# Stick-breaking attention: the sums over later key blocks formed on VectorE, and one product with the matrix of ones per block

## The reference, cut to what matters

```python
z = einsum('bhtd,bhsd->bhts', q, k) * scale          # t: query, s: key
mask = (s_idx < t_idx) & (s_idx >= pad)
log_beta = log_sigmoid(z)
log_rest = where(mask, log_sigmoid(-z), 0.0)
later = cumsum(log_rest, axis=keys, reverse=True) - log_rest   # sum over the keys after s
att = where(mask, exp(log_beta + later), 0.0)
out = einsum('bhts,bhsd->bhtd', att, v)
```

## Time and profile before

| | |
|---|---|
| median of 3 runs | 1735.72 us (1735.57 to 1742.43) |
| profiled execution | 1740.51 us, span 1738.4 us from first to last instruction |
| TensorE products (PE) | busy 1616.3 us, 93% of the span, 16180 instructions |
| DVE, ACT, POOL | 810.9 us (47%), 610.9 us (35%), 162.9 us (9%) |
| attention's pairs | 34 us each while there is fill, seven of them; the eighth has none |

### The profile page before, as it was taken

One profiled execution on the slowest core, in us unless ns is written; L12 is line 12 of the kernel. 1 busy time (PEld: TensorE's weight loads), 2 busy tenths in 40 slices (PEclk: granted clock), 3 DMA queues, 4 the chain that ended last, 5 costly groups with the idle time before them and its releaser, 6 DMA issues. The chain is left out here.

```text
span 1738.4 us, 35740 instructions
## 1 busy us (share of the span) xinstructions
PE 1616.3 (93%) x16180; PEld 1459.7 (84%) x16180; DVE 810.9 (47%) x1098; ACT 610.9 (35%) x827; POOL 162.9 (9%) x186
## 2 busy tenths in 40 slices
PE   4999998899999999979999979888669999999997
PEld 3999987899999999979998968887438888888885
DVE  3455445154442344456766535445485444334432
ACT  2445435242221222236567332233243333122321
POOL 2001001001100011300000321101030010001100
PEclk9999999799999999998999979999889999999998
DMA  3221120122332233332222110000103333323331
GB/s 100 68 62 44 56 64 30 49 86 87 97 105 78 86 89 103 97 116 79 81 70 60 45 52 4 5 4 4 49 22 87 95 90 112 91 86 97 96 99 49
DMA packets 214167, 121.35 MB, mean 70 GB/s; under 512 B 8744, under 2 KB 209600, under 8 KB 213760
## 3 DMA queue, kind: packets, MB, share of 16 engines
q1 hardware_dynamic: 213712, 118.98, 23.3%
q10 hardware_dynamic: 304, 0.08, 0.0%
HBM read 112.29 MB, written 6.76 MB: 68 GB/s over the span
## 5 line engine op out<-in xcount | busy, mean ns | idle before, releaser
L125 ACT ACTIVATE w_hi<-w_raw 128x1024 fp32r<-128x1024 f32 (+1 forms) x194 | 215.9, 1114 | 600.0 <-PE psg L732 481.0
L732 PE MATMUL psg<-x_hi,w_hi 128*128 128x264 f32 (+1 forms) x1096 | 357.2, 326 | 9.3 <-PEq L2469 9.3
L732 PE MATMUL psg<-x_lo,w_hi 128*128 128x264 f32 (+1 forms) x1096 | 357.2, 326 | 0.0
L732 PE MATMUL psg<-x_hi,w_lo 128*128 128x264 f32 (+1 forms) x1096 | 356.4, 325 | 0.0
L129 DVE TENSOR_TENSOR w_lo<-w_raw,w_hi 128x1024 fp32r<-128x1024 f32 (+1 forms) x194 | 250.4, 1291 | 145.5 <-ACT w_hi L125 145.5
L732 PEld LDWEIGHTS psg<-x_hi,w_hi 128*128 128x128 f32 x1096 | 206.2, 188 | 28.8 <-issue 10.3
L732 PEld LDWEIGHTS psg<-x_lo,w_hi 128*128 128x128 f32 x1096 | 206.2, 188 | 18.1 <-issue 0.2
L732 PEld LDWEIGHTS psg<-x_hi,w_lo 128*128 128x128 f32 x1096 | 206.6, 189 | 17.5
L732 PE MATMUL psg<-mid_hi,w_hi 128*128 128x264 f32 (+1 forms) x451 | 146.5, 325 | 0.0
L732 PE MATMUL psg<-mid_lo,w_hi 128*128 128x264 f32 (+1 forms) x451 | 146.3, 324 | 0.0
L732 PE MATMUL psg<-mid_hi,w_lo 128*128 128x264 f32 (+1 forms) x451 | 145.9, 323 | 0.0
(11 more groups left out here) (367 smaller groups left out, 3370.6 us busy)
## 6 DMA issues: line engine op xcount, KB each, us to landing
w_raw<-in_w_ffn_in_dram SPq DMA_DIRECT2D x88, 512.0 KB, 3.8
w_raw<-in_w_ffn_out_dram SPq DMA_DIRECT2D x32, 704.0 KB, 4.6
w_raw<-in_w_qkv_dram SPq DMA_DIRECT2D x24, 512.0 KB, 3.7
w_raw<-in_w_rkv_dram SPq DMA_DIRECT2D x24, 512.0 KB, 3.8
w_raw<-in_w_o_attn_dram SPq DMA_DIRECT2D x8, 512.0 KB, 4.1
w_raw<-in_w_o_rwkv_dram SPq DMA_DIRECT2D x8, 512.0 KB, 3.8
v_first<-v_pair SPq DMA_DIRECT2D x8, 264.0 KB, 2.1
res_kept<-res SPq DMA_DIRECT2D x1, 2112.0 KB, 7.8
```

Source lines behind the costliest of these rows:

```text
L125: k.nc.scalar.activation(k.w_hi[j][:, 0:kt, :], k.raw[j][:, 0:kt, :], ACT.Copy).then_inc(k.hi_ready[j].h, 1)
L732: done = k.nc.tensor.matmul(k.psg[:, 2 * j + c, 0:size], w[:, t, :], x, start=t == first and n == 0, stop=t == last and n == 2)
```

## The change

The far columns of rest are used once more. After rest_low(p, hp) has taken its parts, DVE adds block 4's 16 columns onto the last 16 of block 3, then block 3's 144 onto the last of block 2, then block 2's 272 onto the last of block 1, in place (`later_keys`). Each far block of rest then holds, key by key, the sum over itself and all later blocks. ACT rounds these 864 columns into sum_hi (`sums_high`), DVE makes sum_lo (`sums_low`). TensorE's `later` is cut in two: `own_block` has the products with tri as before, `later_blocks` has for each of four blocks one product with minus on the summed block that follows it, hi and lo, 8 products in place of 20. It waits for sum_lo. Both heads' `own_block` come first, then both heads' `later_blocks`. The diff, with the declarations of semaphores and tiles left out:

```diff
+        def sums_high(p, hp):
+            act.wait_ge(self.add_r.h, 3 * (2 * p + hp + 1))
+            if p:
+                act.wait_ge(self.later_d.h, 2 * (p - 1) + hp + 1)
+            nc.scalar.activation(b.sum_hi[hp][:], b.rest[hp][:, 512:SCORES], ACT.Copy).then_inc(self.shi_r.h, 1)
...
             rest_high(p, 1, 0)
             rest_high(p, 1, 1)
+            sums_high(p, 0)
+            sums_high(p, 1)
...
+        def later_keys(p, hp):
+            n = 2 * p + hp
+            at = [piece_cols(a).start for a in (1, 3, 4, 5)]
+            dve.wait_ge(self.rlo_far.h, n + 1)
+            for step, (to, width, skip) in enumerate(((2, 16, 128), (1, 144, 128), (0, 272, 128))):
+                if step:
+                    dve.wait_ge(self.add_r.h, 3 * n + step)
+                own = b.rest[hp][:, at[to] + skip:at[to] + skip + width]
+                nc.vector.tensor_tensor(own, own, b.rest[hp][:, at[to + 1]:at[to + 1] + width], ALU.add)\
+                    .then_inc(self.add_r.h, 1)
+
+        def sums_low(p, hp):
+            dve.wait_ge(self.shi_r.h, 2 * p + hp + 1)
+            nc.vector.tensor_tensor(b.sum_lo[hp][:], b.rest[hp][:, 512:SCORES], b.sum_hi[hp][:].bitcast(F32),
+                                    ALU.subtract).then_inc(self.slo_r.h, 1)
...
             rest_low(p, 0)
+            later_keys(p, 0)
             softplus(p, 1, 1)
             rest_low(p, 1)
+            later_keys(p, 1)
+            sums_low(p, 0)
+            sums_low(p, 1)
...
-        def later(p, hp):
+        def own_block(p, hp):
...
-            for a, (bank, col, width, key, t0) in enumerate(PIECES):
-                for c, (_, _, width2, key2, t2) in enumerate(PIECES):
-                    if key2 > key and a != 2:
-                        at = col + t2 - t0
-                        for r in (b.rest_hi[hp], b.rest_lo[hp]):
-                            done = mm(ps[:, bank, at:at + width2], b.minus[:], r[:, piece_cols(c)], start=False, stop=True,
-                                      skip_group_check=True)
+        def later_blocks(p, hp):
+            ps = (k.psg, k.psx)[hp]
+            pe.wait_ge(self.slo_r.h, 2 * p + hp + 1)
+            for a, c in ((0, 1), (1, 3), (3, 4), (4, 5)):
+                bank, col, width, key, t0 = PIECES[a]
+                _, _, width2, _, t2 = PIECES[c]
+                at, cols = col + t2 - t0, piece_cols(c)
+                for r in (b.sum_hi[hp], b.sum_lo[hp]):
+                    done = mm(ps[:, bank, at:at + width2], b.minus[:], r[:, cols.start - 512:cols.stop - 512], start=False,
+                              stop=True, skip_group_check=True)
             done.then_inc(self.later_d.h, 1)
...
-            later(p, 0)
-            later(p, 1)
+            own_block(p, 0)
+            own_block(p, 1)
+            later_blocks(p, 0)
+            later_blocks(p, 1)
```

More of the change, by code:

```diff
@@ L200, in __init__ @@
          self.xl_r, self.sq_r, self.acc_r, self.sum_d, self.rs_r, self.half_d, self.half_r, self.z_d, self.clip_r,
-         self.exp_r, self.ln_r, self.rest_r, self.rhi_r, self.rlo_near, self.rlo_far, self.later_d, self.att_r, self.vt_d,
+         self.exp_r, self.ln_r, self.rest_r, self.rhi_r, self.rlo_near, self.rlo_far, self.later_d, self.whole_r, self.add_r, self.shi_r, self.slo_r, self.att_r, self.vt_d,
          self.vt_r, self.out_d, self.ohi_r, self.olo_r, self.v_saved) = (
@@ L205, in __init__ @@
                 "sum", "rstd", "half", "half_read", "z", "clipped", "exp", "ln", "rest", "rest_hi", "lo_near", "lo_far",
-                "later", "att", "v_turned", "v_tok", "out", "o_hi", "o_lo", "v_saved"))
+                "later", "read", "summed", "sums_hi", "sums_lo", "att", "v_turned", "v_tok", "out", "o_hi", "o_lo", "v_saved"))
     def memory(self):
@@ L223, in memory @@
         b.rest_hi, b.rest_lo = ([area.tile(f"rest_{x}{n}", [P, SCORES], F32R) for n in range(2)] for x in ("hi", "lo"))
+        b.sum_hi, b.sum_lo = ([area.tile(f"sum_{x}{n}", [P, SCORES - 512], F32R) for n in range(2)] for x in ("hi", "lo"))
         b.att = b.rest
```

## The result

| | before | changed |
|---|---|---|
| median of 6 runs, us | 1739.86 (1735.57 to 1746.88) | 1768.76 (1760.19 to 1772.22) |
| ratio, 95% interval | | 1.0145 (1.0112 to 1.0177): slower |
| span of the profiled execution | 1738.4 | 1768.7 |
| seven pairs with fill / last pair / all behind attention | 234.6 / 38.7 / 1409.5 | 262.3 / 35.5 / 1414.4 |

The last row is read from the timelines of the one profiled execution of each kernel: a pair reaches from its first product of z to that of the next. The prediction was 1742 us, in a range of 1725 to 1752; the measured 1768.76 lies outside. By the ratio the change costs 25 us (under 2%, but clear of the noise) where 6 were forecast.

The account below looks back on a forecast made before the run. TensorE was taken to bound attention, busy 34.00 of 34 us at full clock. Gains of 8.8 us against 15 us lost to clock falls gave +6 us on 1735.7, so 1742 us, range 1725 to 1752.

Parts of the forecast that it names:

- Part 1: TensorE in attention: 8 minus products a head for 20 remove 2.76 us a middle pair, 5.18 in the last, without waits.
- Part 2: VectorE in attention: three adds a head of 0.17, 0.31 and 0.45 us start the pair's last softplus 1.02 us later.
- Part 3: Middle pairs: TensorE waits 1.82 us for the second head's rest_lo, leaving 0.63 us gain a pair, 4.4 over seven.
- Part 4: Last pair, without fill and at half clock: a gain of 4.4 us, 5.18 less a wait of 0.78.
- Part 5: TensorE's clock in the seven pairs: the wait makes it fall in five, 3.0 us each, 15 us lost.
- rival (b): Seven attention pairs: the clock falls in all at 4.8 us each, +25 us net, 1761 us; chance 0.12.

Follow-up runs that it names:

- e3: The changed kernel with 24 more, useless projection products between the two own blocks in each of seven pairs; 1736.16 us, ratio 0.9984 to the kernel before.
- e2: The changed kernel with POOL's rest_lo of the second head waiting for the first head's three adds; 1757.58 us, ratio 1.0102 to the kernel before.
- e4: The kernel before with only the product order changed: both own blocks first, then all twenty minus products of each head, no adds; 1746.43 us, ratio 1.0036.
- e1: The changed kernel with the first head's adds moved behind the second head's rest_lo on VectorE; 1739.97 us, ratio 1.0003 to the kernel before.
- e6: The changed kernel with the whole half of 24 projection products between the two own blocks, adds left early; 1740.39 us, ratio 1.0000 to the kernel before.
- e8: The changed kernel with adds and sums computed but unused, TensorE running the twenty old products a head in old order; 1741.18 us, ratio 0.9996 to the kernel before.
- e5: e1 with 15 of the 24 projection products that followed the minus products moved between the two own blocks; 1721.80 us, ratio 0.9866 to the kernel before.
- e10: e5 with the first head's adds put back early, beside POOL's rest_lo; 1737.12 us, ratio 0.9968 to the kernel before.
- e7: e6 with the first head's adds behind the second head's rest_lo; 1741.95 us, ratio 0.9995 to the kernel before.

## Why the prediction was wrong

**Part 1 (what TensorE loses) held.** In e3, at full clock, the eight products of a head take 1.08 and 1.09 us (109.22 to 110.30, to 111.39), where the twenty took 2.42 and 2.44: 2.69 us less; 2.76 was forecast.

**Part 2 (the shift by the adds) failed.** Each add alone was priced right (0.17, 0.31, 0.45 against 174, 307, 441 ns) and so was the shift of 1.02 us: it is 1.02 in e2 (from 0.97 to 1.99 us between rest_lo and the softplus, 103.92 to 105.91). In the changed kernel it is 2.01 (105.47 to 108.45). The step that failed is the price of the first head's adds: the prediction asked what they wait for and not what runs beside them. POOL's rest_lo was in the trace of before, then beside a softplus with one operand in PSUM. The rows from which the adds were priced (434 ns for 256 columns) show nothing of this, but the same trace has it in the RWKV stage:

```profile
1028.67 0.68 DVE L2090 TENSOR_TENSOR ar<-xn,w_ext 128x512 f32<-128x512 f32 x1
1028.69 1.78 POOL L2070 TENSOR_TENSOR bk<-kk_in,w_inv 128x512 f32<-128x512 f32 x1
1029.27 1.77 DVE L2091 TENSOR_TENSOR ar<-rr,w_ext 128x512 f32<-128x512 f32 x1
```

L2091 takes 0.68 us where POOL is idle. Of the two operations with both inputs in SBUF here the one that started before POOL's took its usual time and POOL's 0.5 us longer (1.78; it is 1.28 elsewhere); the one that started in the midst of it took 1.77 us and ended 0.57 us after it.

**Part 3 (the wait) had the right place and mechanism**: the second own block waits for rest_lo, 0.80 us by the order (e4: 0.76). Its size was forecast as 1.82 us from the end of the first own block; on the same measure it was 2.81 (111.69 less 107.23, less the 1.65 that the block takes), 0.99 more, which is what Part 2 missed (2.01 less 1.02). (The sum is off by a trifle: 108.65 and the 1.05 us of the second head's products make 109.70 and not 109.75, so 0.68 us a pair and not 0.63.) So what was to be a gain of 0.63 us a pair is a loss of 0.26 (e3) even at full clock.

**Part 4 (the last pair)**: 4.4 us of gain forecast, 3.2 found, 4.7 in e2 and 5.7 in e1: the same term.

**Part 5 (the clock) was mis-sized in both factors.** Five falls at 3.0 us were forecast, 15 us; in the profiled execution it was seven at 3.7, 26 us. The price of 4.8 for the full case was near what e2 shows for its long kind, 4.5. Together: at full clock the stage should have won 8.8 us and wins 1.4 (3.2 less 7 x 0.26), 7.4 us of the miss; the falls are 11 us of it. That makes the 18.5 us between +6 and the +24.5 measured on the eight pairs. Of the other 8 us between the forecast of 1742 and 1768.8, 4 are the base, whose median was 1735.7 us in three runs and is 1739.9 in six; the rest is near the 4.9 us that what lies behind attention took longer in the profiled execution, for a reason that stays open. The forecast's own range was too narrow by the prediction's own terms: it names 3 to 7 falls of 2 to 4.8 us and ends at 1750, but seven at 4.8 make 1761, the time of rival (b), which the outer range of 1725 to 1752 leaves out too.

The rival (b), +25 us, has the measured time, by other terms: falls of 3.7 and not 4.8, and no gain of 8.8 against them. What was wrong in the weighing is the step "5 of the 7 pairs, since thin work surrounds the wait but dense fill stands right before and after": the fill kept the clock up in none of the seven. In the fourth pair it came only 7 us after the wait (185.24 to 192.22), when own block and products with minus had run at half clock. The Trainium skill, "TensorE: Matmul & The Clock Gate", section "HAM oscillation", has each turn of a loop with a wait pay. All seven pairs of the changed kernel did; of the kernels with shorter stops, e2 shows one pair of seven that didn't, e6 two, e1 three.

Missed altogether was what stands in the Trainium skill, "GPSIMD Engine Reference", section "Key points": GpSimd "shares its SBUF interfaces with VectorE", with contention for VectorE instructions that have two inputs in SBUF. That is these adds; the trace agrees, 1415 ns beside POOL and 441 to 443 without.

## What to carry to other kernels

When work is taken off a saturated engine by putting a chain on others, place the chain's end against the moment the engine arrives, then put dense work of the engine itself into the hole; here that turned 1.5% slower into 1.3% faster with the same arithmetic. A short stop of TensorE was dearest here where narrow products followed it: the clock mostly stayed at half through them. Before an operation with two inputs in SBUF is put onto VectorE, look at what POOL does in that very stretch, and look for a row where the two already run side by side.

## What the runs showed of the hardware

- A VectorE add of two SBUF operands beside a two-input POOL instruction: the add of 272 columns, begun 0.28 us after POOL's, ends 0.3 us after it (108.53 and 108.23). Alone it takes 0.44 us, so at most 0.14 of them were done in the 1.12 us beside POOL. The add of 144 columns, begun 0.06 us before POOL's instruction, took its usual 308 ns, and POOL's was 0.1 us longer.
- A fall of TensorE's clock costs by how long it lasts: 1.5 us where the clock came back after 3.4 us (e6, with projections behind the wait), 3.0 and 4.5 us where it came back after 6.8 and 10.2 (e2, with the own block and narrow products behind), after waits of nearly one length (1.77 and 1.69 us). Narrow products with no gap held it at half for 13 us in the last pair of the kernel before, but let it come back after 3.4 us in the changed kernel's second pair.
- Falls in seven pairs, in one execution of each kernel: none with stops of 0.25, 0.57 or 0.66 us (e8, e5, e4), none with 0.73 and, 6 us later, 0.55 (e10); four with 0.66 and 0.98 and the own block between them (e1), six with 1.69 (e2), five and six with 1.77 (e6, e7), seven with 2.66. What decides between pairs of the same kernel stays open.
